# Expert weights in eight places, with a fixed place for each piece of an expert

## What is computed

```python
def ec_moe(x, router_w, w1, w3, w2):
    probs = jax.nn.softmax(jnp.matmul(xf, router_w), axis=-1)
    cap = EC_CAPACITY_FACTOR * N // N_EXPERTS          # 64 of the sample, 16 of the prompt
    gates, idx = lax.top_k(probs.T, cap)
    xe = xf[idx]
    h = jax.nn.silu(jnp.einsum('ecd,edf->ecf', xe, w1)) * jnp.einsum('ecd,edf->ecf', xe, w3)
    ye = jnp.einsum('ecf,efd->ecd', h, w2) * gates[..., None]
    out = jnp.zeros_like(xf).at[idx.reshape(-1)].add(ye.reshape(-1, D))
```

## Time and profile before

| | us |
|---|---|
| median of 3 runs | 1439.09 |
| lowest and highest | 1436.16, 1441.29 |
| the profiled execution | 1439.81 |
| its span, first to last instruction | 1438.0 |

### The profile page before, as it was taken

The page is one execution under the profiler, slowest core; times in us unless marked ns, Lnnn a source line. Parts: engine busy times, 40 slices in busy tenths (PEclk is TensorE's granted clock), DMA queues, the critical chain, the costliest instruction groups (busy, mean ns, idle before and its releaser), DMA issues.

```text
span 1438.0 us, 24229 instructions
## 1 busy us (share of the span) xinstructions
PE 1378.7 (96%) x10891; PEld 565.4 (39%) x10891; DVE 383.0 (27%) x704; ACT 163.1 (11%) x263; POOL 93.3 (6%) x98
## 2 busy tenths in 40 slices
PE   5899999999979999999999999999999999999995
PEld 2354544755533333333333333333333333333331
DVE  2115152533632121303212130321213122120314
ACT  3263323211120000000000000000000000000011
POOL 0200000000001100001000010100001010000000
PEclk8899999999889999999999999999999999999998
DMA  9432312501666999999999999999999999999993
GB/s 357 162 125 101 98 49 111 183 30 59 245 245 259 416 426 419 427 421 416 430 417 427 420 427 421 417 430 416 426 422 426 419 416 430 418 427 419 404 406 123
DMA packets 57773, 470.56 MB, mean 327 GB/s; under 512 B 5317, under 2 KB 7186, under 8 KB 33162
## 3 DMA queue, kind: packets, MB, share of 16 engines
q1 hardware_dynamic: 50816, 451.36, 75.5%
q0 software_dynamic: 6016, 18.17, 4.2%
q10 hardware_dynamic: 906, 0.52, 0.1%
HBM read 456.66 MB, written 13.37 MB: 327 GB/s over the span
## 4 chain that ended last, share of the span: by engine, by line
PE 93%; DVE 3%; DMA 2%; issue 1%; ACT 1%; POOLq 0%; ACTq 0%; POOL 0%; DVEq 0%
PE psum L1035 45%; PE psum L1051 15%; PE psum L685 10%; PE psum L1062 8%; PE psum L898 5%; PE psum L729 2%; PE psum L654 1%; DMA both<-xn_dram,both 1%; PE psum L927 1%; DMA ring<-in_ada_w_dram 1%; PE psum L872 1%; PE psum L876 1%; PE psum L760 0%; PE psum L699 0%; DMA ring<-in_pos_col_dram 0%
## 5 line engine op out<-in xcount | busy, mean ns | idle before, releaser
L1035 PE MATMUL psum<-ring,both 128*32 128x512 f32 x6144 | 664.4, 593 | 0.8 <-DVE both L1747 0.8
L1035 PEld LDWEIGHTS psum<-ring,both 128*32 128x32 f32 x6144 | 238.7, 110 | 419.4 <-issue 416.1
L1051 PE MATMUL psum<-ring,both 128*32 128x512 f32 x2048 | 233.1, 593 | 5.6 <-issue 4.6
L1791 DVE TENSOR_TENSOR both<-both,psum 128x512 f32<-128x512 f32 x48 | 50.3, 1048 | 553.8 <-PE psum L1035 553.8
L685 PE MATMUL psum<-ring,feat 128*128 128x512 f32 x320 | 138.3, 593 | 0.0
L1051 PEld LDWEIGHTS psum<-ring,both 128*32 128x32 f32 x2048 | 78.5, 110 | 150.1 <-issue 150.1
L1334 ACT ACTIVATE both<-psum 128x512 f32<-128x512 f32 x48 | 28.7, 597 | 943.7 <-PE psum L1035 878.5
L1062 PE MATMUL psum<-ring,both 128*32 128x512 f32 x1024 | 120.0, 592 | 0.0
L685 PEld LDWEIGHTS psum<-ring,feat 128*128 128x128 f32 x320 | 60.5, 190 | 76.4 <-issue 76.3
L600 POOL DMA_INDIRECT both<-xn_dram,both x45 | 49.4, 1099 | 578.5 <-DVE both L1802 569.1
L898 PE MATMUL psum<-ring,both 128*128 128x512 f32 x160 | 74.6, 622 | 0.0
(11 more groups left out here) (233 smaller groups left out, 600.7 us busy)
## 6 DMA issues: line engine op xcount, KB each, us to landing
ring<-in_exp_w_dram SPq DMA_DIRECT2D x192, 2048.0 KB, 17.4
ring<-in_ada_w_dram SPq DMA_DIRECT2D x12, 2048.0 KB, 11.4
ring<-in_w_in_dram SPq DMA_DIRECT2D x4, 2048.0 KB, 12.5
ring<-in_w_out_dram SPq DMA_DIRECT2D x2, 2048.0 KB, 9.0
acc_dram<-x POOLq DMA_DIRECT2D x5, 512.0 KB, 2.9
xn_dram<-feat POOLq DMA_DIRECT2D x5, 512.0 KB, 3.0
x<-acc_dram SPq DMA_DIRECT2D x5, 512.0 KB, 14.8
out_dram<-feat SPq DMA_DIRECT2D x5, 512.0 KB, 2.9
```

What stands on the lines that cost most here:

```text
L1035: mm = nc.tensor.matmul(role_bank(role)[f4 * PART:(f4 + 1) * PART, :], xe[:, kt, part * PART:(part + 1) * PART], w[:, kt % 2, f4 * 512:(f4 ...
L1051: mm = nc.tensor.matmul(role_bank("Y_A")[at:at + PART, :], h[:, c, part * PART:(part + 1) * PART], w[:, f, half * 512:(half + 1) * 512], s ...
L1791: role_stored(nc.vector.tensor_tensor(h_rows[:, part, :].rearrange("p (c a) -> p a c", a=PART), silu_h[:, part % 2, :].rearrange("p (a c) ...
```

## The change

Two places are added: tiles 0 to 3 of `x` (place 6, `IN_X`) and of `feat` (place 7, `IN_FEAT`). A piece has the same place in every expert: pieces 0 to 3 and 8 to 11 share slots 3, 4, 5 and 2; piece 4 is in x, 5 in feat, 6 in slot 0, 7 in slot 1. SP's order of loads follows the order in which PE frees places. The reads of x from `acc_dram` come after all pieces. POOL waits for the saves of x before its first gather.

```diff
-EXPERT_SLOT = [3, 4, 5, 2, 0, 1]
-LOADS_BEFORE = [CHUNK_SLOT.count(s) for s in range(RING)]
+IN_X, IN_FEAT = RING, RING + 1
+SHARED_PLACES, OWN_PLACES = [3, 4, 5, 2], [IN_X, IN_FEAT, 0, 1]
+PIECE_SLOT = SHARED_PLACES + OWN_PLACES + SHARED_PLACES
+LOADS_BEFORE = [CHUNK_SLOT.count(s) for s in range(RING + 2)]
...
+def piece_loads(m, expert):
+
+    slot = PIECE_SLOT[m]
+    per_expert = PIECE_SLOT.count(slot)
+    return 16 * (LOADS_BEFORE[slot] + PIECE_SLOT[:m + 1].count(slot)) + expert * (16 * per_expert)
...
         def chunk(slot):
+            if slot == IN_X:
+                return x_all[:, 0:CHUNK_F]
+            if slot == IN_FEAT:
+                return feat[:, 0:CHUNK_F]
             return ring[:, slot * CHUNK_F:(slot + 1) * CHUNK_F]
...
         def wait_expert_chunk(pe, m, expert):
-            slot = EXPERT_SLOT[m % RING]
-            pe.wait_ge(slot_loaded[slot], 16 * (LOADS_BEFORE[slot] + m // RING + 1) + expert * (16 * EXPERT_LOADS // RING))
+            slot = PIECE_SLOT[m]
+            pe.wait_ge(slot_loaded[slot], piece_loads(m, expert))
             return chunk(slot)
...
+            def load_last_four(expert):
+
+                for m in range(8, 12):
+                    wait_expert_chunk_read(sp, m - 8, expert)
+                    load_expert_chunk(m, expert)
+
             wait_filled(sp, JOB["o", TILES - 1])
             sp.wait_ge(o_ready, TILES)
-            for m in range(RING):
-                if m == 3:
-                    wait_trunk_chunk_read(sp, CHUNK_OF["out", 0])
-                    sp.dma_start(chunk(CHUNK_SLOT[CHUNK_OF[ADA[11]]]).rearrange("p (k n) -> p k n", k=KT), ada_k[:, :, 5632:6144])\
-                        .then_inc(slot_loaded[CHUNK_SLOT[CHUNK_OF[ADA[11]]]], 16)
-                if m >= 3:
-                    wait_trunk_chunk_read(sp, chunk_before(EXPERT_SLOT[m], len(TRUNK_CHUNKS)))
+            for m in range(3):
                 load_expert_chunk(m, 0)
-            for m in range(RING, EXPERT_LOADS):
-                wait_expert_chunk_read(sp, m - RING, 0)
+            sp.wait_ge(acc_saved, 16 * ST)
+            sp.wait_ge(xn2_ready, ST)
+            load_expert_chunk(4, 0)
+            sp.wait_ge(xn2_saved, 16 * ST)
+            wait_filled(sp, JOB["hT", ST - 1, 0])
+            wait_filled(sp, JOB["hT", ST - 1, 1])
+            load_expert_chunk(5, 0)
+            wait_trunk_chunk_read(sp, CHUNK_OF["out", 0])
+            sp.dma_start(chunk(CHUNK_SLOT[CHUNK_OF[ADA[11]]]).rearrange("p (k n) -> p k n", k=KT), ada_k[:, :, 5632:6144])\
+                .then_inc(slot_loaded[CHUNK_SLOT[CHUNK_OF[ADA[11]]]], 16)
+            for m in (3, 6, 7):
+                wait_trunk_chunk_read(sp, chunk_before(PIECE_SLOT[m], len(TRUNK_CHUNKS)))
                 load_expert_chunk(m, 0)
-            with sp.Fori(1, LAST) as expert:
-                for m in range(EXPERT_LOADS):
-                    wait_expert_chunk_read(sp, m - RING, expert)
+            load_last_four(0)
+            with sp.Fori(1, EXPERTS) as expert:
+                for m, freed_by in [(m, m) for m in range(4, 8)] + [(m, m + 8) for m in range(4)]:
+                    wait_expert_chunk_read(sp, freed_by, expert - 1)
                     load_expert_chunk(m, expert)
-            for m in range(EXPERT_LOADS):
-                if m == 9:
-                    sp.wait_ge(acc_saved, 16 * (TILES + LAST))
-                    for t in OUT_ORDER:
-                        sp.dma_start(x[:, t, :], acc_dram[t * P:(t + 1) * P, :]).then_inc(acc_loaded[t], 16)
-                wait_expert_chunk_read(sp, m - RING, LAST)
-                load_expert_chunk(m, LAST)
+                load_last_four(expert)
+            sp.wait_ge(w13_read, 6 * EXPERTS)
+            sp.wait_ge(acc_saved, 16 * (TILES + LAST))
+            for t in OUT_ORDER:
+                sp.dma_start(x[:, t, :], acc_dram[t * P:(t + 1) * P, :]).then_inc(acc_loaded[t], 16)
...
             pool.wait_ge(xn2_saved, 16 * ST)
+            pool.wait_ge(acc_saved, 16 * ST)
             pool.wait_ge(slots_ready, 1)
```

More of the change, by code:

```diff
@@ L210, in trunk_kernel @@
         router_amp = sb("router_amp", 2 * KT * EXPERTS)[:].rearrange("p (w k e) -> p w k e", w=2, e=EXPERTS)
-        x = sb("x", TILES * D)[:].rearrange("p (t d) -> p t d", t=TILES)
+        x_all = sb("x", TILES * D)
+        x = x_all[:].rearrange("p (t d) -> p t d", t=TILES)
         feat = sb("feat", TILES * D)
@@ L297, in trunk_kernel @@
         psum_stored = [sem(f"psum_stored{b}") for b in range(BANKS)]
-        slot_loaded = [sem(f"slot_loaded{s}") for s in range(RING)]
+        slot_loaded = [sem(f"slot_loaded{s}") for s in range(RING + 2)]
         extra_loaded = {name: sem(f"extra_loaded_{name}") for name in EXTRA}
@@ L454, in wait_trunk_chunk_read, with wait_expert_chunk_read @@
                 wait_filled(sp, JOB["out", TILES - 1, col // 512])
-        def wait_expert_chunk_read(sp, m, expert):
-            back, m = (1, m + EXPERT_LOADS) if m < 0 else (0, m)
-            when = expert - back
+        def wait_expert_chunk_read(sp, m, when):
             if m < 6:
@@ L522, in load_expert_chunk @@
             def load_expert_chunk(m, expert):
-                slot = EXPERT_SLOT[m % RING]
+                slot = PIECE_SLOT[m]
                 if m < 8:
                     which, k2 = EXPERT_CHUNKS[m]
-                    src = (w1, w3)[which][0, bass.ds(expert, 1)].rearrange("a (p k) n -> p (a k) n", p=P)[:, 2 * k2:2 * k2 + 2, :]
+                    w = (w1, w3)[which][0]
+                    rows = w[bass.ds(expert, 1)] if isinstance(expert, int) else w[1:EXPERTS][bass.ds(expert - 1, 1)]
+                    src = rows.rearrange("a (p k) n -> p (a k) n", p=P)[:, 2 * k2:2 * k2 + 2, :]
                     dst = chunk(slot).rearrange("p (k n) -> p k n", k=2)
```

## The result

| | before, us | changed, us |
|---|---|---|
| median | 1439.95 | 1466.32 |
| lowest and highest | 1436.16, 1441.29 | 1461.37, 1467.93 |
| profiled execution, its span | 1439.81, 1438.0 | 1466.83, 1465.0 |

Four runs each; ratio 1.0182, 95% interval 1.015 to 1.0213. The change costs 26.4 us. The forecast was 1463.5 in a range of 1451 to 1470.

A forecast was written before the change was run, and what follows sets the result against it. The prediction took PE as the bound, with the DMA engines also at their limit in the expert loop. Terms 10.0 + 2.2 + 9.55 + 2.3 = 24.0 us gave 1463.8 or 1463.1, stated as 1463.5, range 1451 to 1470.

The forecast's parts named there:

- Which resource and where: Expert loop: PE and DMA both near their limit; PE idle 0.33 us per expert, no DMA wait to remove.
- Pieces 4 and 5 ahead of the ada columns, +10.0: Before the expert loop: last ada transfer goes sixth instead of fourth in an ordered queue, +10.0 us, bounds 9.8 to 10.6.
- The products at the lower clock, +2.2: Ada product and its turn: run at the lower clock after PE's longer gap, +2.2 us, bounds 0 to 2.6.
- The gather unchanged: First gather, before the loop: stays at 10.19 us, taken as 0, could lose up to 2.2 us.
- Piece 0 of expert 1 is the ninth issue, +9.55: Start of expert 1: piece issued at 470.14 lands at 494.9, PE wants it at 485.39; +9.55 us, bounds 9.2 to 10.0.
- The estimate by the Trainium skill: Start of expert 1: ninth piece would land at 490.6, stall 5.2 us, whole sum 19.3 instead of 24.0.
- The restart, +2.3: Expert 1 after its stall: PE starts at clock 0.50, +2.3 us, bounds 0.3 and 2.5.
- No stall afterwards: Expert 2 onward: first piece lands at 556.2, PE wants it at 559.6; margin 3.4 us, no further stall.
- the growth of that margin by 1.1 us per expert: Experts after 2: the 3.4 us margin of the first piece was to grow by 1.1 us per expert.
- the fall of the age to 7 to 8 us: Issue after the eighth of each burst: landing after about 25 us in expert 1, some 12 in expert 2, then 7 to 8.
- A register instruction more in PE's loop, 0 to 1 us, taken as 0: PE's expert loop: one more register instruction, idle 0.33 us per expert grows by at most a tenth; 0 to 1 us.
- The tail costs nothing: End of the kernel: later x loads land about 1398, before DVE needs x at 1404.6; cost nothing.

The follow-up runs named there:

- e6_one_ahead: Changed kernel with one piece (4) instead of two issued ahead of the last ada columns, piece 5 after them; 1459.98 us (one run).
- e1_ada_first: Changed kernel with the last ada columns issued ahead of pieces 4 and 5 of expert 0; 1454.09 us, 1.0084 of the kernel before.
- e4_piece_wait_first: Changed kernel with PE's wait for piece 8 written ahead of its waits for DVE's transposes; 1468.73 us (one run).
- e7_hold_before: Kernel before the change, with pieces 3 to 5 of expert 0 held until the first gather has landed; 1437.66 us, 0.9981 of the kernel before.

## Why the prediction was right, step by step

- *Which resource and where.* Right. No wait inside the loop was to be removed, none was; the two new waits are at the two places named, 9.0 us before the ada product and 9.55 before expert 1.
- *Pieces 4 and 5 ahead of the ada columns, +10.0.* Right in kind, too large: 8.4, below the lower bound of 9.8. Issued at 378.62 and 379.16, they land at 399.0 and 403.9, 4.9 us apart, and the columns 5.4 after that. The two pieces cost 9.7 us of queue (394.16, where the third piece lands, to 403.85), but before, the columns had been issued only 2.7 us ahead of the queue's end (391.9) and landed 6.6 us after it; now the start of their transfer lies wholly behind other transfers. One of the three piece times had been partly a start-up. I took two full piece times and didn't subtract that. Run e6_one_ahead bears it out: its first piece cost 3.2 us and not 4.9.
- *The products at the lower clock, +2.2.* 2.1. In the changed kernel the granted clock was 0.50 (1.2 GHz) in 406 to 414, with PE idle until 409.30 (8.97 us, where at least 10 was forecast).
- *The gather unchanged.* It was 0.8 shorter (9.37), between 0 and the 2.2 that I had given as its bound.
- *Piece 0 of expert 1 is the ninth issue, +9.55.* Exact: 9.55, and again 9.5 in e1_ada_first and e6_one_ahead. It is the step on which the most depended, and it needed no model of the queue, only the count of issues, because the moments of issue are the same in both kernels. The ninth issue took 24.8 us before and 24.68 now. The estimate by the Trainium skill (page "DMA: Bandwidth & Descriptors", section "Anatomy of one DMA — SWDGE (gpsimd) path") would have made it 5.2 us; this case's trace, with 9.55, does not agree with its size.
- *The restart, +2.3.* Too small: 3.2, above the upper bound of 2.5. The row that the price came from, L898 with 9.19 us, is not a whole restart: PE had been running again since 373.55 with only a short pause, and only the first 4.5 us of that row were at 0.50. Here the clock stayed at 0.50 until 513.4, 6.0 us after PE went on. The first line is of the kernel before, the others of the changed one:

```profile
380.00:385.00 5.00, 5.00 (x8) 2.02 (x7) 4.75 (x11) 0.00 (x0) 0.00 (x0) 0.55 1.02 436
...
500.00:506.00 6.00, 0.00 (x0) 0.00 (x0) 0.00 (x0) 0.00 (x0) 1.20 (x1) 0.76 1.01 404
506.00:508.00 2.00, 0.61 (x4) 0.21 (x8) 0.00 (x0) 0.00 (x0) 0.00 (x0) 0.50 1.06 363
...
512.00:513.00 1.00, 1.00 (x8) 0.20 (x4) 0.00 (x0) 0.00 (x0) 0.00 (x0) 0.50 0.96 410
513.00:514.00 1.00, 1.00 (x12) 0.26 (x8) 0.00 (x0) 0.00 (x0) 0.00 (x0) 0.81 1.07 459
```

  What a restart costs is not a constant. Four profiles have this stall, of 9.5 to 9.7 us, and the time that the chain gives to the 368 matmuls behind it, 39.52 at the full clock, was 42.69, 42.49 (e4_piece_wait_first), 42.40 (e1_ada_first) and 41.16 (e6_one_ahead). The clock was back 6.0, 5.6, 5.4 and 2.9 us after PE went on, so the price was 3.2, 3.0, 2.9 and 1.6 us, about half of the time spent at 0.50.
- *No stall afterwards.* Right. Piece 0 of expert 2 is issued at 557.77 and lands after 10.4 us (12 expected), 4.9 us before PE wants it at 573.05, where a margin of 3.4 was forecast. What did not come is the growth of that margin by 1.1 us per expert, and the fall of the age to 7 to 8 us: piece 0 of expert 3 lands after 10.7 us with 4.6 to spare, and the median age over the run is 10. Nothing hung on it, since no later expert waits.
- *A register instruction more in PE's loop, 0 to 1 us, taken as 0.* Too small: 1.9 us in the account, above its bound of 1, of which the experiment ties about 1.4 (0.09 to 0.10 per expert) to the instruction's place behind the transposes' wait. The row was in the order of PE's program; I had looked at how many such instructions there are and not at where they stand.
- *The tail costs nothing.* Right: the x loads are issued at 1416.1 to 1417.9, land in time for ACT at 1424.7, and DVE is done with x by 1437.7, before the last matmuls end at 1444.2.
- *The trunk.* 2.4 us of the 27.0 have nothing to do with the change. In 269 to 279 the granted clock was 1.00 in the profile of before and 0.56 in that of after. Run e7_hold_before, whose program is that of before up to 396 us, shows 0.50 there, and its ada columns are issued at 393.31. All ten profiles line up by the granted clock in 264 to 282: at 0.91 the columns are issued at 389.14 and 389.21, at 0.72 at 390.06 and 390.16, at 0.62 to 0.63 between 391.10 and 391.83, and at 0.53 between 392.92 and 393.31, whichever kernel it is. How much of the spread from run to run comes from this stretch is not shown; it goes with the clock, though: of the 26 runs of the kernel before, the fastest (1434.03) had a mean granted clock of 0.988 and the slowest (1445.73) of 0.974. Single differences of 2 us are therefore not explained here.

By the medians, 1466.32 is 2.8 above the forecast: the terms of the change itself, without the trunk's 2.4, sum to 24.6 where 24.0 was forecast, with misses of -1.6, -0.1, -0.8, +0.3, +0.9 and +1.9 that nearly cancel. Three of these terms lay outside their own bounds, so that the sum comes within 0.6 us is luck; that the two delays stand where they were placed, and that the larger one is exact, is not.

## What to carry to other kernels

Where one queue feeds an engine and is served in order, more places do not mean a longer lead for every piece: count, for each piece, how many issues stand ahead of it in the new order, and read its landing from the old trace at that count. Load what is wanted next before what only has room, but do not let the queue run empty to do so: putting off four pieces cost 130 us against the order of the change, putting off two saved 10.4. And look for small transfers on the critical chain that share the DMA engines with large ones which could start later.

## What the runs showed of the hardware that I had not expected

- A gather of 64 rows of 4 KB took 10.2 us beside three queued pieces of 2 MB and 4.2 us without them, though it is issued on another queue than they are.
- A gap of 4.2 us was enough for the 16 matmuls of the ada product to run nearly as slowly (3.35 us) as after 9.0 us (3.64), against 1.97 after a gap of 0.9 us. After the same stall of 9.5 to 9.7 us the clock was back 2.9 to 6.0 us after the restart, which made the price of the restart anything from 1.6 to 3.2 us.
- The same trunk program reached the ada issue at times 4.1 us apart in different executions (389.21 and 393.31), and the granted clock in 264 to 282 (0.91 and 0.53) orders these times in all ten profiles.
- The wait for a piece, with the register instruction that its value needs, costs 0.09 to 0.10 us each time that it stands behind a wait on another engine and not ahead of it.
